# The first two weight units and x arrive in parts from two issuing queues and are rounded block by block; two more units are split before x's squares and the Silu table

## The chip, the cores and the metric

One core of one Trainium2 chip runs the whole program. The metric is the device time of one execution in microseconds (us); the kernel before takes 1129.0 us, the median of three runs.

## The reference, cut to what matters

Two transformer blocks in float32 on 256 rows of 1024 features. The change touches only the very first operation, a SwiGLU feed-forward layer behind an RMS norm:

```python
def rmsnorm(x, g):
    xf = x.astype(jnp.float32)
    y = xf * lax.rsqrt(jnp.mean(xf * xf, axis=-1, keepdims=True) + EPS)
    return y.astype(x.dtype) * g

def swiglu(x, w_gate, w_up, w_down):
    return (jax.nn.silu(x @ w_gate) * (x @ w_up)) @ w_down

h = h + 0.5 * rmsnorm(swiglu(rmsnorm(h, ffn1_pre_g[l]), ffn1_w_gate[l], ffn1_w_up[l], ffn1_w_down[l]),
                      ffn1_post_g[l])
```

with `w_gate` and `w_up` of 1024 x 2816 and `w_down` of 2816 x 1024. Behind it stand a state-space and an attention branch, a second feed-forward layer, and a second block with two attentions and a third such layer. The change leaves all of that as it is.

## The kernel before

**Split products.** Every float32 operand of a large product is held as two float32r parts, high (a rounded copy, made by ScalarE, ACT below) and low (the rest, made by VectorE, DVE below). A product is then three matmuls: high by high, high by low, low by high. The weights come in 180 *units* of 128 x 2048 values (1 MB each), which stand in a ring of five slots. For each unit SyncE (SP) issues the load into RAW (`load`, L363), ACT writes the high part WH (`split_hi`, L454, 461) and DVE the low part WL (`split_lo`, L1007, 1014); WL lies over RAW. A slot is loaded again once TensorE (PE) has counted the unit in `w_used`. Each engine runs its own instructions strictly in order, so their order in the text decides what waits for what.

**The first layer.** Unit 0 holds rows 0 to 511 of the first 256 columns of `w_gate` and `w_up` (two loads of 512 KB), as four row blocks k of 128 x 512; unit 1 holds rows 512 to 1023 of the same columns. Units 2 and 3 are the next 256 columns of gate and of up, unit 4 is the first 256 rows of `w_down`; then gate, up and down follow in turn.

**The start.** x lies in H as two row tiles t of 128 rows. For each tile and each half q of its features PE transposes four blocks (`turn_normed`, L1610, 1621); ACT multiplies them by the norm's gain into the high part XTH (`x_hi`, L612, 617) and DVE makes the low part XTL (`x_lo`, L1188, 1194). Both signal only after the last of the four. Four such quarters, (t, q) = (0, 0), (0, 1), (1, 0) and (1, 1), fill XT. PE's `first_norm` (L1867) multiplies: unit 0 by tile 0, block by block (12 matmuls, with tile 1's two transposes between), unit 0 by tile 1 (12), unit 1 by tile 0 (12), unit 1 by tile 1 (12). ACT's order is table load, x quarters (0, 0) and (0, 1), unit 0, squares of tile 0, x quarter (1, 0), unit 1, x quarter (1, 1), squares of tile 1, the Silu table, unit 2. The squares (`h_rstd`, L474, 483 to 485) give each row's norm factor, which is applied behind the products (L523 on ACT, L1063 on DVE); the result, the first 256 hidden columns, is transposed on PE in `turn_hidden` (L1757, 1762; L1767 turns the row factors).

**The loop.** For each later step j of `ffn` (L1736) PE multiplies the gate unit by all rows, as two blocks of 16 matmuls (`block`, L1740: L1753 with 512 columns, L1755 with 256), then the up unit likewise, then the down unit of the step before (24 matmuls, L1695 to 1697). In step 1 `turn_hidden` stands between the two blocks of unit 2. ACT splits units 3 and 4 around the copy of the turned hidden values (L527), and unit 5 behind them.

## Time and profile before

| | |
|---|---|
| runs | 1129.0, 1130.46 and 1128.63 us, median 1129.0 |
| the profiled execution | 1128.79 us, span 1127.0 us |
| PE busy | 1110.2 us (99% of the span) |
| DVE busy | 772.7 us (69%) |
| ACT busy | 618.7 us (55%) |
| DMA | 202.28 MB, 179 GB/s over the span |

A row of the timeline gives the start, the duration, the engine, the line and operation, what it writes and reads, how many were merged (x8), and in brackets the idle time of the engine before it and what ended that. Names ending in q are an engine's queue of DMA issues. Operations of an engine overlap a little: the next starts before the duration of the last is over, so that the pace is read from starts. The times of the table are the device's; those of the rows count from the span's first instruction.

### The profile page before, as it was taken

What the parts mean: (1) busy time and instruction counts of PE and PEld (TensorE: products, weight loads), DVE (VectorE), ACT (ScalarE), POOL (GpSimd) and SP (SyncE); (2) the same over time, 40 slices, a digit from 0 to 9 for tenths busy, and PEclk for the clock granted to TensorE, in tenths of its full rate; (3) what the DMA queues carried; (4) which work ended last, traced back from release to release, by engine and by line L of the source; (5) the groups of instructions that cost most, each with busy time, mean ns of one, the idle gap of its engine ahead of it and who ended that gap; (6) DMA issues with size and microseconds to landing.
All of it is one profiled execution on the core that took longest, in us unless ns stands there. A gap on an engine that the chain in (4) does not pass through costs nothing.

```text
span 1127.0 us, 14916 instructions
## 1 busy us (share of the span) xinstructions
PE 1110.2 (99%) x6114; PEld 949.8 (84%) x6114; DVE 772.7 (69%) x904; ACT 618.7 (55%) x877; POOL 20.9 (2%) x34
## 2 busy tenths in 40 slices
PE   6999999999999999999999999999999999999997
PEld 5888888999999987788888888888878888888886
DVE  4766667676767777868768666675775667766664
ACT  6644445554567766655456444456766546444443
POOL 0000000000001100000000000000000000000000
PEclk9999999999999999999999999999999999999999
DMA  8765564755566545345565655545633445555550
GB/s 280 249 191 189 187 191 136 229 187 179 178 205 192 167 166 205 118 157 192 177 218 182 193 187 189 193 147 154 221 124 119 168 151 187 186 187 188 186 187 38
DMA packets 131395, 202.28 MB, mean 179 GB/s; under 512 B 4944, under 2 KB 98000, under 8 KB 131072
## 3 DMA queue, kind: packets, MB, share of 16 engines
q1 hardware_dynamic: 128656, 190.68, 52.1%
q0 software_dynamic: 2672, 10.65, 2.8%
q8 instruction: 49, 0.80, 0.3%
q14 instruction: 18, 0.15, 0.0%
HBM read 200.24 MB, written 1.08 MB: 179 GB/s over the span
## 4 chain that ended last, share of the span: by engine, by line
PE 93%; DVE 4%; ACT 2%; issue 1%; DMA 0%; SPq 0%; DVEq 0%; ACTq 0%
PE TOP L1753 20%; PE ACC L1695 14%; PE ACC L1697 13%; PE ACC L1696 13%; PE TOP L1755 10%; PE TOP L1695 5%; PE TOP L1697 4%; PE TOP L1696 4%; DVE WL L1014 1%; ACT WH L461 1%; PE ACC L1973 1%; PE TOP L1621 1%; PE TOP L2131 1%; PE TOP L1818 1%; PE TOP L2139 0%
## 5 line engine op out<-in xcount | busy, mean ns | idle before, releaser
L1014 DVE TENSOR_TENSOR WL<-RAW,WH 128x2048 fp32r<-128x2048 f32 (+2 forms) x180 | 406.5, 2263 | 108.6 <-ACT WH L461 108.1
L461 ACT ACTIVATE WH<-RAW 128x2048 fp32r<-128x2048 f32 (+2 forms) x180 | 339.1, 1890 | 73.2 <-DMA RAW<-in_ffn_w_gate 30.7
L1753 PE MATMUL TOP<-XT,WH 128*128 128x512 f32 x960 | 340.4, 399 | 0.0
L1755 PE MATMUL TOP<-XT,WL 128*128 128x256 f32 x960 | 269.5, 281 | 0.0
L1753 PEld LDWEIGHTS TOP<-XT,WH 128*128 128x128 f32 x960 | 180.4, 188 | 44.9 <-DVE WL L1014 0.5
L1755 PEld LDWEIGHTS TOP<-XT,WL 128*128 128x128 f32 x960 | 181.3, 189 | 1.0
L1695 PE MATMUL ACC<-WH,KTH 128*128 128x512 f32 (+1 forms) x452 | 179.3, 397 | 0.0
L1697 PE MATMUL ACC<-WH,KTL 128*128 128x512 f32 (+1 forms) x452 | 176.0, 389 | 0.0
L1696 PE MATMUL ACC<-WL,KTH 128*128 128x512 f32 (+1 forms) x452 | 175.5, 388 | 0.0
L506 ACT ACTIVATE SCR<-TOP 128x512 f32<-128x512 f32 x60 | 35.8, 596 | 165.7 <-PE TOP L1755 165.7
L1697 PEld LDWEIGHTS ACC<-WH,KTL 128*128 128x128 f32 x452 | 84.8, 188 | 18.5
L1695 PEld LDWEIGHTS ACC<-WH,KTH 128*128 128x128 f32 x452 | 84.9, 188 | 18.2 <-DVE KTL L1169 0.7
L1696 PEld LDWEIGHTS ACC<-WL,KTH 128*128 128x128 f32 x452 | 85.0, 188 | 15.6
L1047 DVE TENSOR_TENSOR SCR<-TOP,SCR 128x512 f32<-128x512 f32 x60 | 41.4, 691 | 79.6 <-ACT SCR L506 79.6
L1695 PE MATMUL TOP<-WH,XT 128*128 128x512 f32 (+1 forms) x200 | 80.2, 401 | 4.5 <-DVE WL L1204 3.3
L1697 PE MATMUL TOP<-WH,XT 128*128 128x512 f32 (+1 forms) x200 | 78.0, 390 | 0.0
L1696 PE MATMUL TOP<-WL,XT 128*128 128x512 f32 (+1 forms) x200 | 77.8, 389 | 0.0
L1695 PE MATMUL ACC<-XT,WH 128*128 128x256 f32 x208 | 60.0, 289 | 0.0
L1696 PE MATMUL ACC<-XT,WH 128*128 128x256 f32 x208 | 59.6, 286 | 0.0
L1697 PE MATMUL ACC<-XT,WL 128*128 128x256 f32 x208 | 59.5, 286 | 0.0
L1695 PE MATMUL ACC<-WH,XT 128*128 128x512 f32 (+1 forms) x144 | 56.3, 391 | 0.7 <-DVE WL L1014 0.6
L1697 PE MATMUL ACC<-WH,XT 128*128 128x512 f32 (+1 forms) x144 | 54.2, 377 | 0.0
(304 smaller groups left out, 1449.9 us busy)
## 6 DMA issues: line engine op xcount, KB each, us to landing
RAW<-in_w_in SPq DMA_DIRECT2D x50, 1024.0 KB, 5.2
RAW<-in_ffn_w_down SPq DMA_DIRECT2D x22, 1024.0 KB, 4.9
RAW<-in_ffn_w_gate SPq DMA_DIRECT2D x20, 1024.0 KB, 5.4
RAW<-in_ffn_w_up SPq DMA_DIRECT2D x20, 1024.0 KB, 5.4
RAW<-in_w_down SPq DMA_DIRECT2D x11, 1024.0 KB, 4.9
RAW<-in_w_gate SPq DMA_DIRECT2D x10, 1024.0 KB, 5.4
RAW<-in_w_up SPq DMA_DIRECT2D x10, 1024.0 KB, 5.3
RAW<-in_ssd_w_branch SPq DMA_DIRECT2D x8, 1024.0 KB, 4.8
```

The lines of the kernel that those rows point to most:

```text
L461: nc.scalar.activation(WH[:, s, 0:n], RAW[:, s, 0:n], ACT.Copy).then_inc(w_hi, 1)
L506: nc.scalar.activation(LOW[n], TOP[:, bank:bank + 2, TOK:2 * TOK], ACT.Copy).then_inc(low_kept, 1)
L1014: tt(WL[:, s, 0:n], RAW[:, s, 0:n], WH[:, s, 0:n].bitcast(F32), ALU.subtract).then_inc(w_lo, 1)
L1047: tt(by_block(dst), TOP[:, bank:bank + 2, 0:TOK], LOW[n], ALU.add).then_inc((gate_sum, up_sum)[n], 1)
L1621: ins = nc.tensor.transpose(PS[6 + q][:, k * P:(k + 1) * P], src[:, t, j * P:(j + 1) * P], IDENT)
L1695: mm(ps, stat_hi, mov_hi, start=first, stop=False)
L1696: mm(ps, stat_hi, mov_lo, start=False, stop=False)
L1697: return mm(ps, stat_lo, mov_hi, start=False, stop=last)
L1753: mm(PS[bank], WH[:, slot(c), ws], XT[:, k, :, :].rearrange("p u t -> p (u t)"), start=k == 0, stop=False)
L1755: ins = mm(PS[bank][:, TOK:2 * TOK], WL[:, slot(c), ws], XTH[:, k, :], start=False, stop=k == KD - 1)
L1818: ins = nc.tensor.transpose(PS[7][:, k * P:(k + 1) * P], src[:, t, (k0 + k) * P:(k0 + k + 1) * P], IDENT)
L1973: ins = mm(PS[3][:, e * SSD_P:(e + 1) * SSD_P], DECAY[n % 2][:, e, :], XDT[:, e * SSD_P:(e + 1) * SSD_P], start=True, stop=True)
```

## The change

- **Loads.** x's tile 0 comes as two halves of its features, unit 0 as four row blocks (gate and up part of each), unit 1 as two halves. SP issues the first half of x, the four gate blocks, x's tile 1 and unit 1. ACT, which issued no DMA before, issues the identity matrix, the gains, the four up blocks and the second half of x ahead of its table load. The bytes are the same.
- **Rounding in turn.** ACT and DVE treat block k of x's quarter (0, 0) and block k of unit 0 one after the other, each with its own signal; the four turned blocks lie in four PSUM banks. PE starts on a block when both parts of it are there.
- **Transposes.** Each quarter has a place of its own in PSUM (`x_turned_at`). Quarter (0, 1) is turned behind block 1, quarter (1, 0) behind block 3, and quarter (1, 1) behind the first half of unit 1's product with tile 0.
- **Order.** ACT's squares of both tiles, which stood before and behind x's quarters, come behind unit 2's split, and unit 3's split comes before the Silu table. In the first layer `turn_hidden` stands behind both blocks of unit 2.

```diff
+LOADS[0] = LOADS[1] = 0
...
-        x_loaded = [sem(f"x_loaded{t}") for t in range(NT)]
+        x_loaded = [[sem("x_loaded0_first"), sem("x_loaded0_second")], [sem("x_loaded1")]]
+        first_loaded = [sem(f"first_unit_loaded{k}") for k in range(4)]
+        second_loaded = [sem(f"second_unit_loaded{h}") for h in range(2)]
+        second_hi, second_lo, x_first = sem("second_unit_hi"), sem("second_unit_lo"), sem("first_rows_hi")
+        x_first_lo = sem("first_rows_lo")
         loaded, tab_loaded, stored = sem("loaded"), sem("tables_loaded"), sem("stored")
...
+        def x_turned_at(t, k):
+            if t == 0 and k < 4:
+                return PS[(6, 7, 2, 3)[k]][:, 0:P]
+            return PS[{(0, 1): 0, (1, 0): 1, (1, 1): 6}[t, k // 4]][:, k % 4 * P:(k % 4 + 1) * P]
...
-            sp.dma_start(H[:, 0, :], x_in[:, 0, :]).then_inc(x_loaded[0], 16)
-            sp.dma_start(IDENT, w["tables"][:, 0:P]).then_inc(ident_loaded, 16)
-            sp.dma_start(COLS[:, 0:KD], w["cols"][:, 0:KD]).then_inc(ident_loaded, 16)
+            sp.dma_start(H[:, 0, 0:512], x_in[:, 0, 0:512]).then_inc(x_loaded[0][0], 16)
+            for k in range(4):
+                sp.dma_start(RAW[:, 0, k * 512:k * 512 + 256],
+                             w["ffn1_w_gate"][k * P:(k + 1) * P, 0:256]).then_inc(first_loaded[k], 16)
+            sp.dma_start(H[:, 1, :], x_in[:, 1, :]).then_inc(x_loaded[1][0], 16)
+            for h in range(2):
+                part = RAW[:, 1, h * 1024:(h + 1) * 1024].rearrange("p (k c) -> p k c", c=512)
+                for n, src in enumerate((w["ffn1_w_gate"], w["ffn1_w_up"])):
+                    sp.dma_start(part[:, :, n * 256:(n + 1) * 256],
+                                 src[512 + 256 * h:768 + 256 * h, 0:256].rearrange("(k p) c -> p k c", p=P)
+                                 ).then_inc(second_loaded[h], 16)
...
                 nc.scalar.activation(KTH[:, half_of(0)], PS[3], ACT.Copy).then_inc(hT_hi, 1)
-                split_hi()
+                if f:
+                    split_hi()
...
-            def first_unit_hi():
-                act.wait_ge(raw[0], 16 * LANDED[next(splits)])
+            def first_hi_parts():
+                next(splits)
+                act.wait_ge(ident_loaded, 32)
+                act.wait_ge(xn_turned, 1)
                 for k in range(4):
+                    ins = nc.scalar.activation(XTH[:, k, 0:P], x_turned_at(0, k), ACT.Copy, scale=COLS[:, k:k + 1])
+                    ins.then_inc(x_first, 1) if k < 3 else ins.then_inc(xt_hi, 1)
+                    act.wait_ge(first_loaded[k], 32)
                     a = slice(k * 512, (k + 1) * 512)
                     ins = nc.scalar.activation(WH[:, 0, a], RAW[:, 0, a], ACT.Copy)
                     ins.then_inc(first_hi, 1) if k < 3 else ins.then_inc(w_hi, 1)
+            def second_unit_hi():
+                next(splits)
+                for h in range(2):
+                    act.wait_ge(second_loaded[h], 32)
+                    a = slice(h * 1024, (h + 1) * 1024)
+                    nc.scalar.activation(WH[:, 1, a], RAW[:, 1, a], ACT.Copy).then_inc(w_hi if h else second_hi, 1)
+            act.dma_start(IDENT, w["tables"][:, 0:P]).then_inc(ident_loaded, 16)
+            act.dma_start(COLS[:, 0:KD], w["cols"][:, 0:KD]).then_inc(ident_loaded, 16)
+            for k in range(4):
+                act.dma_start(RAW[:, 0, k * 512 + 256:(k + 1) * 512],
+                              w["ffn1_w_up"][k * P:(k + 1) * P, 0:256]).then_inc(first_loaded[k], 16)
+            act.dma_start(H[:, 0, 512:1024],
+                          w["x"].rearrange("o (t p) d -> p (o t) d", p=P)[:, 0, 512:1024]).then_inc(x_loaded[0][1], 16)
             ln_exp()
-            x_hi(0, 0)
+            first_hi_parts()
             x_hi(0, 1)
-            first_unit_hi()
+            x_hi(1, 0)
+            second_unit_hi()
+            x_hi(1, 1)
+            split_hi()
             h_rstd(0, 0)
-            x_hi(1, 0)
+            h_rstd(0, 1)
             split_hi()
-            x_hi(1, 1)
-            h_rstd(0, 1)
             nc.scalar.preload_act_table(ACT.Silu)
-            split_hi()
             ffn(0, U_FFN1)
...
-            def first_unit_lo():
+            def first_lo_parts():
                 next(splits)
+                dve.wait_ge(ident_loaded, 32)
                 for k in range(4):
+                    dve.wait_ge(x_first, k + 1) if k < 3 else dve.wait_ge(xt_hi, 1)
+                    ins = stt(XTL[:, k, 0:P], x_turned_at(0, k), COLS[:, k:k + 1], XTH[:, k, 0:P].bitcast(F32),
+                              ALU.mult, ALU.subtract)
+                    ins.then_inc(x_first_lo, 1) if k < 3 else ins.then_inc(xt_lo, 1)
                     a = slice(k * 512, (k + 1) * 512)
                     dve.wait_ge(first_hi, k + 1) if k < 3 else dve.wait_ge(w_hi, 1)
                     ins = tt(WL[:, 0, a], RAW[:, 0, a], WH[:, 0, a].bitcast(F32), ALU.subtract)
                     ins.then_inc(first_lo, 1) if k < 3 else ins.then_inc(w_lo, 1)
-            x_lo(0, 0)
+            def second_unit_lo():
+                next(splits)
+                for h in range(2):
+                    dve.wait_ge(w_hi, 2) if h else dve.wait_ge(second_hi, 1)
+                    a = slice(h * 1024, (h + 1) * 1024)
+                    tt(WL[:, 1, a], RAW[:, 1, a], WH[:, 1, a].bitcast(F32), ALU.subtract).then_inc(w_lo if h else second_lo, 1)
+            first_lo_parts()
             x_lo(0, 1)
-            first_unit_lo()
             x_lo(1, 0)
+            second_unit_lo()
+            x_lo(1, 1)
             split_lo()
-            x_lo(1, 1)
             split_lo()
             ffn(0, U_FFN1)
...
+            def turn_input(t, q):
+                pe.wait_ge(x_loaded[t][-1 if t else q], 16)
+                if t and q:
+                    pe.wait_ge(xt_lo, 1)
+                for k in range(4 * q, 4 * q + 4):
+                    ins = nc.tensor.transpose(x_turned_at(t, k), H[:, t, k * P:(k + 1) * P], IDENT)
                 ins.then_inc(xn_turned, 1)
...
                     block(c, 0, 6)
-                    if j == 1:
+                    if j == 1 and f:
                         turn_hidden()
                     block(c, 1, 7).then_inc(w_used, 1)
+                    if j == 1 and not f:
+                        turn_hidden()
...
             def first_norm(c):
                 for k in range(4):
-                    pe.wait_ge(first_lo, k + 1) if k < 3 else pe.wait_ge(w_lo, c + 1)
-                    pe.wait_ge(xt_lo, 1)
+                    if k < 3:
+                        pe.wait_ge(first_lo, k + 1)
+                        pe.wait_ge(x_first_lo, k + 1)
+                    else:
+                        pe.wait_ge(w_lo, c + 1)
+                        pe.wait_ge(xt_lo, 1)
                     half(c, 0, 0, 4, (k,))
-                    if k % 2:
-                        turn_normed(0, 1, k // 2)
+                    if k == 1:
+                        turn_input(0, 1)
+                turn_input(1, 0)
                 pe.wait_ge(xt_lo, 3)
                 half(c, 0, 1, 5).then_inc(w_used, 1)
+                pe.wait_ge(second_lo, 1)
+                pe.wait_ge(xt_lo, 2)
+                half(c + 1, 1, 0, 4, (0, 1))
+                turn_input(1, 1)
                 pe.wait_ge(w_lo, c + 2)
-                half(c + 1, 1, 0, 4).then_inc(chunk_half, 1)
+                half(c + 1, 1, 0, 4, (2, 3)).then_inc(chunk_half, 1)
                 pe.wait_ge(xt_lo, 4)
                 half(c + 1, 1, 1, 5).then_inc(w_used, 1)
             pe.wait_ge(ident_loaded, 32)
-            first_tile(0)
+            turn_input(0, 0)
```

**ACT, from the program's start to the splits behind x's quarters, before** (XT is x's high part, WH the weights', SS the sums of squares):

```order
L472 ACT_TABLE_LOAD
L617 ACTIVATE XT<-TOP,COLS 128x128 x8
L626 ACTIVATE WH<-RAW 128x512 x4
L483 ACTIVATE SCR,SS<-H 128x1024
...
L617 ACTIVATE XT<-TOP,COLS 128x128 x4
L461 ACTIVATE WH<-RAW 128x2048
L617 ACTIVATE XT<-TOP,COLS 128x128 x4
...
L638 ACT_TABLE_LOAD
L461 ACTIVATE WH<-RAW 128x2048
L523 ACTIVATE SCR<-TOP,RS 128x256 x2
```

**The same stretch of ACT now** (between the first pair of block and unit block and the last stand two more such pairs):

```order
L666 DMA RAW<-in_ffn_w_up 128x256 x4
L668 DMA H<-in_x 128x512
L492 ACT_TABLE_LOAD
L648 ACTIVATE XT<-TOP,COLS 128x128
L652 ACTIVATE WH<-RAW 128x512
...
L638 ACTIVATE XT<-ACC,COLS 128x128 x8
L661 ACTIVATE WH<-RAW 128x1024 x2
L638 ACTIVATE XT<-TOP,COLS 128x128 x4
L481 ACTIVATE WH<-RAW 128x2048
...
L481 ACTIVATE WH<-RAW 128x2048
L680 ACT_TABLE_LOAD
L544 ACTIVATE SCR<-TOP,RS 128x256 x2
```

Seven DMA issues (two of them are those of the identity and the gains) stand ahead of the table load. The last quarter of x (the row L638 with x4) stands ahead of unit 2's split (the first L481); the squares stand between the two L481, and the second L481 is unit 3.

**PE, around the second product of unit 0, before** (WH and WL with XT are products, TAB with H are transposes):

```order
L1697 MATMUL TOP<-WH,XT 128x512
L1621 MATMUL TOP<-TAB,H 128x128 [waits xt_lo,x_loaded1]
L1621 MATMUL TOP<-TAB,H 128x128 x3
L1695 MATMUL TOP<-WH,XT 128x512 [waits xt_lo,first_unit_lo]
...
L1695 MATMUL TOP<-WH,XT 128x512 [waits xt_lo,weights_lo]
L1696 MATMUL TOP<-WL,XT 128x512
L1697 MATMUL TOP<-WH,XT 128x512
L1621 MATMUL TOP<-TAB,H 128x128 [waits xt_lo,x_loaded1]
L1621 MATMUL TOP<-TAB,H 128x128 x3
L1695 MATMUL TOP<-WH,XT 128x512 [waits xt_lo]
```

**PE, the same place and unit 1's first product now:**

```order
L1754 MATMUL TOP<-WH,XT 128x512 [waits xt_lo,weights_lo]
L1755 MATMUL TOP<-WL,XT 128x512
L1756 MATMUL TOP<-WH,XT 128x512
L1680 MATMUL ACC<-TAB,H 128x128 [waits x_loaded1]
L1680 MATMUL ACC<-TAB,H 128x128 x3
L1754 MATMUL TOP<-WH,XT 128x512 [waits xt_lo]
...
L1754 MATMUL TOP<-WH,XT 128x512 [waits xt_lo,second_unit_lo]
...
L1680 MATMUL TOP<-TAB,H 128x128 [waits xt_lo,x_loaded1]
L1680 MATMUL TOP<-TAB,H 128x128 x3
L1754 MATMUL TOP<-WH,XT 128x512 [waits weights_lo]
```

Before, the transposes of quarter (1, 0) had six products and another four transposes between them and the product that waits for that quarter (`xt_lo`). Now they stand directly ahead of it. The transposes of quarter (1, 1) have moved behind six products of unit 1.

## Rows read from the trace of the kernel before

**Rows 1.** The page's busy times, and PE's longest wait past 20 us.

```profile
PE 1110.2 (99%) x6114; PEld 949.8 (84%) x6114; DVE 772.7 (69%) x904; ACT 618.7 (55%) x877; POOL 20.9 (2%) x34
PE ACC L1695 <- DVE WL L1014: 0.6, 1, 0.6
```

**Rows 2.** The timeline of PE, 0 to 32 us.

```profile
4.83 1.97 PE L1621 MATMUL TOP<-TAB,H 128*128 128x128 f32 x8 [4.83 <-DMA COLS<-in_cols]
10.12 0.80 PE L1695 MATMUL TOP<-WH,XT 128*128 128x512 f32 x1 [3.31 <-DVE WL L1204]
...
15.14 0.60 PE L1621 MATMUL TOP<-TAB,H 128*128 128x128 f32 x4
16.42 0.50 PE L1695 MATMUL TOP<-WH,XT 128*128 128x512 f32 x1 [0.68 <-DVE XT L1194]
19.32 0.50 PE L1695 MATMUL TOP<-WH,XT 128*128 128x512 f32 x1
...
25.09 0.50 PE L1753 MATMUL TOP<-XT,WH 128*128 128x512 f32 x1
27.97 0.60 PE L1762 MATMUL ACC<-TAB,SCR 128*128 128x128 f32 x4
28.54 0.48 PE L1753 MATMUL TOP<-XT,WH 128*128 128x512 f32 x1
31.44 0.40 PE L1753 MATMUL TOP<-XT,WH 128*128 128x512 f32 x1
```

**Rows 3.** The chain of waits from 0 to 32 us: start, duration, what.

```profile
4.83 1.13 PE TOP L1621 x4
6.05 1.15 ACT XT L617 x4
9.46 0.61 DVE WL L1204
12.62 0.43 PE TOP L1697
14.00 1.15 ACT XT L617 x4
16.92 0.23 PE TOP L1696
```

**Rows 4.** The timeline of ACT.

```profile
8.47 2.19 ACT L626 ACTIVATE WH<-RAW 128x512 fp32r<-128x512 f32 x4 [0.24 <-DMA RAW<-in_ffn_w_up]
17.82 1.11 ACT L483 ACTIVATE SCR<-H 128x1024 f32<-128x1024 f32 x1
19.50 1.28 ACT L638 ACT_TABLE_LOAD   x1
20.79 1.92 ACT L461 ACTIVATE WH<-RAW 128x2048 fp32r<-128x2048 f32 x1
```

**Rows 5.** The timeline of DVE.

```profile
22.74 2.29 DVE L1014 TENSOR_TENSOR WL<-RAW,WH 128x2048 fp32r<-128x2048 f32 x1 [2.44 <-ACT WH L461]
49.13 0.69 DVE L1047 TENSOR_TENSOR SCR<-TOP,SCR 128x512 f32<-128x512 f32 x1 [2.13 <-ACT SCR L506]
```

**Rows 6.** The timeline of SP's queue, seventh to ninth issue.

```profile
3.69 0.43 SPq L370 DMA_DIRECT2D RAW<-in_ffn_w_gate  x1
4.17 0.78 SPq L370 DMA_DIRECT2D RAW<-in_ffn_w_up  x1
4.99 0.97 SPq L370 DMA_DIRECT2D RAW<-in_ffn_w_gate  x1
```

**Rows 7.** DMA issues by line: count, KB each, us from issue to landing.

```profile
H<-in_x SPq DMA_DIRECT2D x1, 512.0 KB, 3.6
RAW<-in_ffn_w_up SPq DMA_DIRECT2D x1, 512.0 KB, 5.9
H<-in_x SPq DMA_DIRECT2D x1, 512.0 KB, 6.6
COLS<-in_cols SPq DMA_DIRECT2D x1, 4.0 KB, 3.1
```

More of the change, by code:

```diff
@@ L384, in ffn_loads @@
                 for n, (kind, j) in enumerate(FF):
-                    if kind == "d":
+                    if u0 == U_FFN1 and n < 2:
+                        pass
+                    elif kind == "d":
                         load(u0 + n, down[j * 256:(j + 1) * 256, :], D)
@@ L390, in ffn_loads @@
                         gate_up(u0 + n, "ab".index(kind), j, gate, up)
-                    if u0 == U_FFN1 and n == 0:
-                        sp.dma_start(H[:, 1, :], x_in[:, 1, :]).then_inc(x_loaded[1], 16)
                     if u0 == U_FFN1 and n == 6:
@@ L478, in h_rstd @@
                 else:
-                    act.wait_ge(x_loaded[t], 16)
+                    for part in x_loaded[t]:
+                        act.wait_ge(part, 16)
                 own.wait() if own.n else None
@@ L612, in x_hi @@
             def x_hi(t, q):
-                act.wait_ge(ident_loaded, 32)
                 act.wait_ge(xn_turned, 2 * t + q + 1)
                 for k in range(4 * q, 4 * q + 4):
-                    ins = nc.scalar.activation(XTH[:, k, t * P:(t + 1) * P], PS[6 + q][:, k % 4 * P:(k % 4 + 1) * P],
-                                               ACT.Copy, scale=COLS[:, k:k + 1])
+                    ins = nc.scalar.activation(XTH[:, k, t * P:(t + 1) * P], x_turned_at(t, k), ACT.Copy,
+                                               scale=COLS[:, k:k + 1])
                 ins.then_inc(xt_hi, 1)
-            def first_unit_hi():
-                act.wait_ge(raw[0], 16 * LANDED[next(splits)])
+            def first_hi_parts():
+                next(splits)
+                act.wait_ge(ident_loaded, 32)
+                act.wait_ge(xn_turned, 1)
                 for k in range(4):
+                    ins = nc.scalar.activation(XTH[:, k, 0:P], x_turned_at(0, k), ACT.Copy, scale=COLS[:, k:k + 1])
+                    ins.then_inc(x_first, 1) if k < 3 else ins.then_inc(xt_hi, 1)
+                    act.wait_ge(first_loaded[k], 32)
                     a = slice(k * 512, (k + 1) * 512)
@@ L1069, in ffn @@
                 nc.vector.tensor_copy(RSB, PS[2][:, 0:TOK]).then_inc(rsb_ok, 1)
-                split_lo()
+                if f:
+                    split_lo()
                 dve.wait_ge(rsb_ok, f + 1)
@@ L1610, in turn_normed @@
             def turn_normed(n, t, q):
[L1612 to L1615 removed]
+                pe.wait_ge(xn_ok, 4 * (n - 1) + 2 * t + q + 1)
                 if t:
                     pe.wait_ge(xt_lo, 4 * n + q + 1)
[L1618 removed]
                 for k in range(4):
                     j = 4 * q + k
[L1621 removed]
+                    ins = nc.tensor.transpose(PS[6 + q][:, k * P:(k + 1) * P], XN[:, t, j * P:(j + 1) * P], IDENT)
+                ins.then_inc(xn_turned, 1)
+            def turn_input(t, q):
[4 more added lines that the diff above has]
+                    ins = nc.tensor.transpose(x_turned_at(t, k), H[:, t, k * P:(k + 1) * P], IDENT)
                 ins.then_inc(xn_turned, 1)
```

11 lines of the change are left out of this document (2 added, 9 removed).

## The prediction

> **What bounds the kernel now.** I read the page's busy times first: PE works 1110.2 of 1127.0 us [rows 1]. So nearly any time comes from what PE waits for, and the list of PE's waits says where that is: its longest wait past the first 20 us is 0.6 us [rows 1]; the rest is at the start. There the timeline of PE shows three gaps [rows 2]: 4.83 us until the gains (COLS) have landed, 3.31 us between the transposes and the first product at 10.12 us, and 0.68 us at 16.42, before unit 0's second product. At 25.09 the loop's first block starts, and unit 3 at 31.44. The chain of waits then says what fills the second gap [rows 3]: ACT's quarter of x (1.15 us), DVE's quarters, and the low part of one unit block (0.61 us). From 31.44 on nothing is changed but PE's start and how far ACT and DVE are behind it. So the question is one number: when does PE start unit 3?
>
> **To the first product.** The gains are now ACT's second DMA. SP's eighth issue starts at 4.17 [rows 6], the first at 0.74, which is 0.49 us each; so the gains are issued at about 1.2 and land 3.1 us later [rows 7], at 4.3. The first half of x is half of a transfer that landed after 3.6 us [rows 7], and is there too. PE starts at 4.3 instead of 4.83. ACT must first issue seven DMAs, until 0.74 + 7 x 0.49 = 4.17, and load its table, 1.28 us [rows 4]: ready at 5.45. The four transposes take 1.22 us (4.83 to 6.05 in the chain [rows 3]): 5.52. The two meet almost exactly, and ACT starts on x at 5.5, against 6.05.
>
> Then one block of x (a quarter of 1.15 us), one block of unit 0 (2.19 us for four [rows 4], so 0.55), its low part and the hand-over (9.46 to 10.12 [rows 2, 3], 0.66), and about 0.1 us for the wait between: PE's first product starts at 5.5 + 0.29 + 0.55 + 0.1 + 0.66 = 7.1. That is 3.0 us earlier. The next blocks follow every 0.87 us on DVE (0.27 for x, 0.6 for the unit), while PE needs 1.28 us for the three matmuls of a block at 0.43 each [rows 3], so PE is not held again here.
>
> Have the data landed by then? The loads share one stream of bytes, so I go by bytes: x's tile 0 (512 KB) landed at 0.74 + 3.6 = 4.34; with the identity and both parts of unit 0, 1.6 MB had landed at 2.59 + 5.9 = 8.5 [rows 7]. On the line between these two, block 0 (complete with 580 KB) lands at 4.6 and block 3 (1.35 MB) at 7.5; if parts lag behind their bytes, up to 1 us later. ACT wants them at 5.8 and 8.2. Close, but within the line. x's second half is wanted at 9.8 and comes by about 9; x's tile 1, issued by SP at about 3.1 as before, lands 6.6 us later [rows 7] and is wanted at 12.1.
>
> **To unit 0's second product.** PE does the same twelve matmuls and four transposes as before, and those of the next quarter: 10.12 to 15.14 [rows 2] is 5.02 us, with PE's clock at its lower level for the first part: steps of 0.43 us for 512 columns are 1.2 GHz, and the later ones of 0.23 are 2.4 GHz [rows 3]. The clock rose about 3.4 us after 10.12. I take the same course from the new start. Quarter (1, 0) is then turned from 7.1 + 5.0 = 12.1 to 12.7 (0.60 us [rows 2]). Here is the price of the new order. Before, that quarter's way over ACT and DVE (14.00 to 16.42 [rows 2, 3], 2.42 us) ran beside six products and four transposes, and PE stood 0.68 us. Now nothing stands between: ACT starts at 12.8, and PE resumes at 15.2. PE idles 2.5 us. Of the 3.0 us won, 1.2 are left.
>
> **To unit 2.** Twelve matmuls take 2.8 us (24 from 19.32 to 24.9 [rows 2], 0.23 each): 18.0. Unit 1's two halves are split well before (ACT 13.9 to 15.9). Six matmuls of unit 1: 19.4. Only now quarter (1, 1) is turned, and ACT, in order, has waited for it since 15.9. ACT gets it at 20.0, is through at 21.15, and only then starts unit 2: 1.92 us [rows 4] and DVE's 2.29 us [rows 5] end at 25.4 to 25.5. Before, ACT started unit 2 at 20.79 [rows 4]. PE for its part finishes six matmuls at 21.3, waits for the quarter until 20.0 + 2.42 = 22.4, and ends at 25.3. It starts unit 2 at 25.5, where it started at 25.09. **The lead is gone, and 0.4 us with it**: a whole quarter and a whole unit's split now hang in series behind a late transpose.
>
> **To unit 3.** Behind unit 2's split ACT has two rounds of squares of 1.7 us (17.82 to 19.50 with the two small steps [rows 4]), unit 3 (1.82), and the table (1.28): 23.1 + 3.4 + 1.8 + 1.3 = 29.6. Two scaled copies and DVE's two products bring the hidden values to 31.4. PE has both blocks of unit 2 behind it at 25.5 + 2.88 + 2.8 = 31.2 [rows 2] and waits 0.2 us. The transposes take 0.57 us (27.97 to 28.54) as before: unit 3 starts at 32.0 instead of 31.44. Had the transposes stayed between the blocks, PE would have stood 3 us; the move of them is worth that, and is counted. The split of unit 3 before the table costs nothing on PE: its low part is ready at 30.5.
>
> **Behind it.** DVE comes out of the squares' delay late: unit 4's low part ends at 34.4, the turned hidden values and row factors at 35.4. PE wants them at 32.0 + 5.65 = 37.6. So 2 us of cover are left, and DVE, which waited 2.13 us before the next sum [rows 5], catches up. I cost this at nothing; if it failed, what it costs is the overrun alone.
>
> **The sum.** +0.6 us at unit 3, and nothing later. The profiled execution took 1128.79 us (its span and 1.8 us around it), 0.2 below the median of 1129.0. So 1128.79 + 0.6 = **1129.4 us**. A measurement of this kernel can tell about 0.2%, 2.3 us, from no change: within that the change is none.
>
> A rule that speaks against this change in itself: the Trainium skill, page "DMA: Bandwidth & Descriptors", section "Issuing engines are not separate DMA queues", says that DMAs of several issuing engines run on the same 16 engines and that a second issuer saves only the sequencer's time. By that rule the second queue is worth at most the issues that it takes off SP; the trace of before has one issuer and can't show it.
>
> **The rivals.**
> - *ACT's issues are slow* (the other side, slower). SP's eighth and ninth issue took 0.78 and 0.97 us [rows 6]. Above 0.50 us each, the table load ends behind the transposes, and each further 0.1 us costs 0.7 us, undiminished, since the whole chain to unit 2 hangs on it. At 0.80 us each: table ready at 7.6, +2.1 us, 1131.5 us. Against it: SP's first seven kept to 0.49 with fewer bytes in flight. 10%.
> - *The parts land late.* Even 4 KB took 3.1 us [rows 7], so small transfers save little, and two queues share the engines. Blocks 0.3 to 1 us later give 1129.7 to 1130.4. 15%. The same page's section "Bandwidth" says that small transfers run at a fraction of the rate of one of 1 MB, which points this way.
> - *The clock rises sooner.* PE now stands 1.6 us between transposes and products instead of 3.3. If it multiplies at 2.4 GHz from the start, six matmuls save 0.2 us each, the transposes 0.35 and the fill 0.2, together 1.7 us. They go through to unit 2: 1127.7 us. 12%.
> - *The clock stays or falls low in the new gap* of 2.5 us. Eighteen matmuls at 0.43 instead of 0.23 are +3.6 us, half of that if it recovers midway: 1131.2 to 1133. Against it: the gap of 0.68 us left the clock up; none of this length stands behind a rise in the trace. 8%.
> - *The lead survives.* If the late quarter didn't hold unit 2 (its hand-over shorter than the 2.42 us of before), unit 2 could start at PE's own end without gaps, 1.2 to 2 us earlier: 1127.5 us. 7%.
>
> **How the numbers follow.** My forecast has 48%, with 1128.8 to 1130.2 as its own range (starts spread by the clock's rise). From 1127.5 (the two faster cases) to 1131.2 (late parts, and the lower part of the slow cases) about 17% is left out. Faster by over 0.2% (below 1126.8) needs two of the gains at once: 6%. Slower by over 0.2% (above 1131.2): half of the slow issues and most of the low clock, 12%. Within: 82%.
>
> **What would show it.** In the profile after, in this order: the first transpose at 4.3; ACT's table load ending by 5.5; the first product near 7.1; a gap of PE of about 2.5 us before unit 0's second product, released by DVE's low part of x; ACT idle some 4 us until about 20 for the last quarter; a gap of 1.1 us on PE before unit 1's second product; unit 2 at 25.5, a short gap before `turn_hidden`, and unit 3 at 32.0. A table load that ends after 6, steps of 0.43 us behind the gap, or unit 3 before 31 would prove me wrong.

## The result and the profile after

The changed kernel takes **1131.82 us** (median of 16 executions, 1128.48 to 1136.77); the kernel before, timed beside it, 1128.91 us (16 executions). The ratio is 1.0023, with a 95% interval of 1.0015 to 1.0031: slower by some 2.9 us, where 0.6 was forecast. The range ended at 1131.2.

The profiled execution took 1131.33 us (span 1129.7). The page's busy times and the list of PE's waits, after:

```profile
PE 1111.9 (98%) x6114; PEld 950.7 (84%) x6114; DVE 773.0 (68%) x905; ACT 619.0 (55%) x878; POOL 20.9 (2%) x34
PE TOP L1680 <- DMA COLS<-in_cols: 4.4, 1, 4.4
PE TOP L1754 <- DVE XT L1235: 3.4, 2, 2.4
PE TOP L1754 <- DVE WL L1250: 2.0, 1, 2.0
```

Before, the start cost PE 4.8, 3.3 and 0.7 us of waiting, 8.8 together [rows 2]. Now it costs 4.4, 2.0 and 3.4, which is 9.8: all that the early product won is waited for again behind it, and 1 us more. Besides, PE is busy for 1.7 us longer than before [rows 1], with the same 6114 matmuls. Two causes, then: waiting, and a lower clock. The timeline of PE after, for [rows 2]:

```profile
4.38 0.69 PE L1680 MATMUL TOP<-TAB,H 128*128 128x128 f32 x2 [4.38 <-DMA COLS<-in_cols]
...
7.48 0.79 PE L1754 MATMUL TOP<-WH,XT 128*128 128x512 f32 x1 [1.98 <-DVE WL L1250]
...
10.50 1.12 PE L1680 MATMUL ACC<-TAB,H 128*128 128x128 f32 x4
...
12.96 0.60 PE L1680 MATMUL ACC<-TAB,H 128*128 128x128 f32 x4
...
15.95 0.50 PE L1754 MATMUL TOP<-WH,XT 128*128 128x512 f32 x1 [2.39 <-DVE XT L1235]
...
20.19 0.60 PE L1680 MATMUL TOP<-TAB,H 128*128 128x128 f32 x4
...
23.18 0.50 PE L1754 MATMUL TOP<-WH,XT 128*128 128x512 f32 x1 [0.99 <-DVE XT L1235]
...
26.14 0.50 PE L1812 MATMUL TOP<-XT,WH 128*128 128x512 f32 x1
...
31.90 0.60 PE L1821 MATMUL ACC<-TAB,SCR 128*128 128x128 f32 x4
...
32.48 0.48 PE L1812 MATMUL TOP<-XT,WH 128*128 128x512 f32 x1
```

PE multiplies 2.64 us earlier (7.48 against 10.12), has 0.47 us left at unit 0's second product (15.95 against 16.42), is 1.05 us late at unit 2 (26.14 against 25.09) and 1.04 us late at unit 3 (32.48 against 31.44). The timeline of ACT after, for [rows 4], shows how the late transposes hold unit 2:

```profile
4.08 1.28 ACT L492 ACT_TABLE_LOAD   x1 [4.08 <-issue]
...
9.41 0.63 ACT L652 ACTIVATE WH<-RAW 128x512 fp32r<-128x512 f32 x1 [0.60 <-DMA RAW<-in_ffn_w_up]
11.66 1.14 ACT L638 ACTIVATE XT<-ACC,COLS 128x128 fp32r<-128x128 f32 x4 [1.62 <-PE ACC L1680]
...
20.83 1.14 ACT L638 ACTIVATE XT<-TOP,COLS 128x128 fp32r<-128x128 f32 x4 [4.20 <-PE TOP L1680]
21.84 1.93 ACT L481 ACTIVATE WH<-RAW 128x2048 fp32r<-128x2048 f32 x1
```

ACT stands idle 4.20 us for the quarter that PE turns at 20.19, and unit 2, for which it needs nothing from PE, waits behind it: 21.84, where it began at 20.79 before [rows 4].

The other 1.7 us lie far behind the change. Stretches of 10 us before (first two rows) and after (last two): the number ahead of the DMA share (0.93, 0.90) is the granted clock of PE as a share of 2.4 GHz. (Ahead of the clock's first rise this column shows 1.00, although the steps of 0.43 us for 512 columns are those of 1.2 GHz. The mean clocks of the executions agree with this column, so they don't count that time either; there the clock is read from the steps.)

```profile
210.00:220.00 10.00, 10.00 (x63) 9.18 (x62) 7.03 (x9) 6.25 (x8) 0.00 (x0) 0.93 0.68 225
220.00:230.00 10.00, 10.00 (x78) 10.00 (x78) 9.22 (x25) 5.66 (x7) 0.00 (x0) 0.90 0.61 197
```

```profile
210.00:220.00 10.00, 10.00 (x53) 8.73 (x53) 5.25 (x4) 4.21 (x4) 0.00 (x0) 0.84 0.44 140
220.00:230.00 10.00, 10.00 (x73) 10.00 (x73) 8.46 (x27) 7.22 (x10) 0.00 (x0) 0.83 0.72 218
```

There, behind a unit whose products are only 32 columns wide, the clock went down from 2.4 to 1.2 GHz once before (0.07 x 10 + 0.10 x 10 = 1.7 us lost) and twice after (1.6 + 1.7 = 3.3 us). PE never idles in these stretches. 1.0 us from the start and 1.7 us from here make up the whole difference of the two spans, 2.7 us.

But this profile is one execution. Is the second low stretch the change's doing? The experiments speak against it: what the change does to the clock happens in the start, and this profile happens not to show it.

### The profile page after: what moved, and what is told of

Read it like the earlier page. It is cut to its first block, busy times and chain, and to the rows that moved or that the text cites. A ratio compares the mean times of both kernels' runs of the same rounds, so it can differ in the third digit from the quotient of the medians.

```text
span 1129.7 us, 14922 instructions
## 1 busy us (share of the span) xinstructions
PE 1111.9 (98%) x6114; PEld 950.7 (84%) x6114; DVE 773.0 (68%) x905; ACT 619.0 (55%) x878; POOL 20.9 (2%) x34
## 4 chain that ended last, share of the span: by engine, by line
PE 92%; DVE 3%; ACT 2%; issue 1%; DMA 1%; ACTq 0%; DVEq 0%
PE TOP L1812 20%; PE ACC L1754 14%; PE ACC L1756 13%; PE ACC L1755 13%; PE TOP L1814 10%; PE TOP L1754 5%; PE TOP L1755 4%; PE TOP L1756 4%; DVE WL L1055 1%; ACT WH L481 1%; PE ACC L2043 1%; PE TOP L2201 1%; DMA H<-in_x 1%; PE TOP L1671 1%; PE TOP L1879 1%
## 5 line engine op out<-in xcount | busy, mean ns | idle before, releaser
L481 ACT ACTIVATE WH<-RAW 128x2048 fp32r<-128x2048 f32 (+2 forms) x179 | 337.3, 1889 | 71.6 <-DMA RAW<-in_ffn_w_gate 29.7
```

The lines of the kernel that those rows point to most:

```text
L481: nc.scalar.activation(WH[:, s, 0:n], RAW[:, s, 0:n], ACT.Copy).then_inc(w_hi, 1)
```

## The experiments

The theory at first: the late transposes (PE order) hold unit 2, and the lower clock is what the new times of things do to the narrow products. Rivals: the second queue delivers its parts late; the new gap of 2.4 us lets the clock fall in the start. The table holds every run, with what its profile shows at three places: the start of unit 3 (in kernels that keep `turn_hidden` between unit 2's blocks it is left out), whether the granted clock fell in the first 40 us after its first rise, and how many low stretches there are between 210 and 230 us. Each ratio is to the kernel before, timed in the same set of runs (medians of 1128.5 to 1128.9 us). All ratios lie within 1% of 1; what is told apart here are tenths of a percent, and only where the intervals do it.

| run | median us (executions) | ratio, 95% interval | span | unit 3 | fell in the start | low at 210 to 230 |
|---|---|---|---|---|---|---|
| before | 1129.0 (3) | | 1127.0 | 31.44 | no | 1 |
| after | 1131.82 (16) | 1.0023, 1.0015 to 1.0031 | 1129.7 | 32.48 | no | 2 |
| a_again | 1132.85 (4) | 1.0038, 1.0025 to 1.0052 | 1131.2 | 36.54 | yes | 0 |
| a_third | 1132.94 (10) | 1.0035, 1.0022 to 1.0048 | 1134.7 | 37.41 | yes | 2 |
| b_mixed | 1129.62 (12) | 1.0009, 0.9996 to 1.0022 | 1128.1 | | no | 0 |
| a_mixed | 1133.71 (7) | 1.0029, 1.0015 to 1.0043 | 1132.4 | 36.18 | yes | 0 |
| b_late_gains | 1131.32 (11) | 1.0018, 1.0009 to 1.0026 | 1129.5 | | no | 1 |
| a_turn_early | 1130.52 (12) | 1.0001, 0.9989 to 1.0013 | 1126.0 | 30.36 | no | 1 |
| a_filled | 1133.51 (6) | 1.0032, 1.0020 to 1.0044 | 1132.7 | 35.55 | no | 1 |
| a_one_queue | 1131.22 (10) | 1.0012, 1.0002 to 1.0021 | 1126.6 | 32.20 | no | 0 |
| a_hold | 1131.55 (10) | 1.0018, 1.0009 to 1.0027 | 1129.8 | 33.79 | yes | 1 |
| a_swap | 1127.25 (11) | 0.9980, 0.9970 to 0.9989 | 1124.4 | 29.84 | no | 0 |
| a_swap_again | 1125.60 (11) | 0.9977, 0.9965 to 0.9988 | 1123.9 | 29.26 | no | 0 |
| a_swap_one_queue | 1129.08 (11) | 0.9998, 0.9989 to 1.0007 | 1127.9 | 32.27 | no | 1 |
| a_swap_x_on_act | 1128.26 (12) | 1.0000, 0.9991 to 1.0009 | 1127.1 | 30.91 | no | 1 |
| b_late_turn | 1136.45 (4) | 1.0072, 1.0054 to 1.0090 | 1134.8 | | yes | 2 |
| a_hidden_between | 1136.91 (4) | 1.0065, 1.0049 to 1.0082 | 1134.8 | | twice | 1 |

The columns add up: 1127.0 + (unit 3 - 31.44) + 1.7 x (low stretches - 1) gives the span of ten of the eleven rows with a start of unit 3 (a_mixed, whose later products differ, left aside) within 0.8 us, and that of a_filled within 1.6. So between unit 3 and the end the number of low stretches is the only large difference; the up to 0.8 us that is left (1.6 in a_filled) stays open.

**The narrow products, taken out.** In both kernels the narrow matmuls (`beside`) were put between wide ones, in small groups:

```diff
-                    half(c + 1, 1, 0, 4).then_inc(chunk_half, 1)
-                    pe.wait_ge(w_lo, c + 3)
-                    beside(0)
...
+                        pe.wait_ge(w_lo, c + 3)
+                        for k in range(4):
+                            ins = half(c + 1, 1, 0, 4, (k,))
+                            if k == 3:
+                                ins.then_inc(chunk_half, 1)
+                            beside(0, (2 * k, 2 * k + 1))
```

> The kernel before, with the 48 narrow products (32 columns) of the dt unit mixed among the wide ones of unit 1 of the mixer instead of standing in two blocks of 24. If the low clock near 220 us comes from those two blocks (theory 1), its profile shows no low stretch there and its runs gather near 1127 us, 1.7 us below the kernel before. If the low stretch is chance or belongs to another place (theory 2), time and clock stay as before, 1128.9 us, 0.998.

> The changed kernel with the same mixing. Theory 1: the clock stays high, the runs lose their spread, and what is left against the kernel before with the same mixing is the start alone, +0.8 to +1.0 us: about 1128 us. Theory 2 (the 2.7 us all come from the start or from the queues): it stays near 1131.8 us.

Neither profile has a low stretch at 210 to 230 us. One profile each doesn't show that the mixing did it, since four profiles without it (a_again, a_one_queue, a_swap, a_swap_again) have none there either. The mean clocks say more: 8 of b_mixed's 12 executions have 0.999 or 1.000, against 5 of 30 of the kernel before in the same set. But two of the twelve have 0.993 and are 6 us longer (1135.4 and 1135.8 us); where the clock fell in them no profile shows. The kernel before stays level instead of the 1.7 us faster that were expected: the narrow products had covered the split of the next unit, and the list of PE's waits of b_mixed has a new one, whose longest part stands directly ahead of them:

```profile
PE TOP L1713 <- DVE WL L1014: 1.7, 2, 1.5
205.28 0.47 PE L1713 MATMUL TOP<-WH,XT 128*128 128x512 f32 x1 [1.54 <-DVE WL L1014]
```

The changed kernel doesn't come closer: 4.1 us above b_mixed (1133.71 against 1129.62). So the second low stretch of the profile after was not the cause. Of a_mixed's seven executions two have a span of 1128.4 and 1128.5 us at a mean clock of 0.999, five have 1131.1 to 1133.0 at 0.998. The profiled one (1132.4) is of the five, and its clock fell in the start, behind the gap. A fall costs 1.7 us, so it can explain less than half of the 4 us between the two groups. The rest is lost in another way, and the next two profiles show how that can be.

**The changed kernel once more**, unchanged, in two other sets of runs:

> The changed kernel once more, for a second profile and more runs on the chip of this call. Theory 1: another trace may show a low stretch within the first 25 us; unit 2 starts between 25.9 and 28. Theory 2: none does, and the clock differs from run to run only by the stretches near 210 and 220 us.

> The changed kernel a third time, for one more profile of its start. From the profiles so far: the up blocks land 4.9 or 6.5 us after their issue, and the clock falls back in the gap in about two executions of three; unit 2 then starts at 26, 27 or 30 us.

Both profiles show what the first did not. PE's timeline of a_third, two stretches of 2 us in it, and two rows of a_again:

```profile
10.14 0.80 PE L1754 MATMUL TOP<-WH,XT 128*128 128x512 f32 x1 [1.12 <-DVE WL L1250]
...
12.37 1.12 PE L1680 MATMUL ACC<-TAB,H 128*128 128x128 f32 x4 [0.57 <-DMA H<-in_x]
...
15.84 1.05 PE L1680 MATMUL ACC<-TAB,H 128*128 128x128 f32 x4
19.29 0.50 PE L1754 MATMUL TOP<-WH,XT 128*128 128x512 f32 x1 [2.39 <-DVE XT L1235]
...
28.12 0.50 PE L1754 MATMUL TOP<-WH,XT 128*128 128x512 f32 x1 [1.01 <-DVE XT L1235]
...
37.27 0.38 PE L1826 MATMUL ACC<-TAB,RS 128*128 128x128 f32 x2
```

```profile
20.00:22.00 2.00, 2.00 (x7) 1.57 (x6) 1.50 (x2) 0.00 (x0) 0.00 (x0) 0.55 0.16 64
22.00:24.00 2.00, 2.00 (x7) 1.51 (x7) 0.00 (x0) 0.00 (x0) 0.00 (x0) 0.60 0.02 6
```

```profile
14.91 0.63 PE L1756 MATMUL TOP<-WH,XT 128*128 128x512 f32 x1
15.34 0.68 PE L1680 MATMUL ACC<-TAB,H 128*128 128x128 f32 x4
```

First, block 1 and x's second half come late: quarter (0, 1) is turned at 12.37 (a_again: 11.87), at 10.50 in the first profile. Second, the clock's first rise comes late too. In the first profile the steps are at 0.23 us from 11.80 on, 4.3 us behind the first product. In a_again they stand at 0.43 up to the transposes at 15.34, 8.2 us behind it, and in a_third the same four transposes still take 1.05 us at 15.84. The six products and four transposes from quarter (0, 1) to quarter (1, 0) so take 3.5 us in both instead of 2.5 (12.96 - 10.50). What sets the rise wasn't tested. In both profiles PE had stood 0.6 to 1.1 us twice since its first product, but in a_swap_again (below), where it stood for nothing, the steps are also at 0.43 us up to 12.97, 5.7 us behind the first product. Third, the clock is at 1.2 GHz behind the gap of 2.39 us: 0.45 x 2 + 0.40 x 2 = 1.7 us. Together unit 3 starts 5 to 6 us later than before, 4.1 and 4.9 us later than in the first profile. Of these the fall is 1.6 to 1.7 us; most of the rest is the late parts and the late rise, which together cost more than the fall in these two profiles.

**A later start alone.** In the kernel before, identity and gains issued behind unit 0's loads:

```diff
                     if u0 == U_FFN1 and n == 0:
+                        sp.dma_start(IDENT, w["tables"][:, 0:P]).then_inc(ident_loaded, 16)
+                        sp.dma_start(COLS[:, 0:KD], w["cols"][:, 0:KD]).then_inc(ident_loaded, 16)
...
-            sp.dma_start(IDENT, w["tables"][:, 0:P]).then_inc(ident_loaded, 16)
-            sp.dma_start(COLS[:, 0:KD], w["cols"][:, 0:KD]).then_inc(ident_loaded, 16)
```

> The kernel before with the identity and the gains issued behind unit 0's loads, so that the whole program from the first transpose on starts about 0.9 us later, nothing else moved. If a later start alone brings the second low stretch near 210 us (the phase is tied to the start of the program), +2.6 us and clock 0.996. If the phase is free from run to run, +0.9 us and the same share of low stretches as before.

The shift came out larger than meant: the 4 KB of gains, issued behind 1 MB of weights, landed only at 7.9 us instead of 4.8. Everything moved by 3 us and the kernel lost 2.4, but the mean clock of its executions (0.9984) was no lower than that of before (0.9977). Here being late cost its own time, and the clock didn't fall more often.

**The order of the transposes.** Three kernels change it. a_turn_early turns quarter (1, 1) right behind (1, 0); a_swap also exchanges quarters (1, 0) and (0, 1) on PE, ACT and DVE, so that a whole product stands between the transposes and the product that waits for them (PE's part of the edit of a_swap; ACT and DVE take the two quarters in the same order):

```diff
                     if k == 1:
-                        turn_input(0, 1)
-                turn_input(1, 0)
-                pe.wait_ge(xt_lo, 3)
+                        turn_input(1, 0)
+                turn_input(0, 1)
+                turn_input(1, 1)
+                pe.wait_ge(xt_lo, 2)
                 half(c, 0, 1, 5).then_inc(w_used, 1)
...
-                turn_input(1, 1)
```

> The changed kernel with the last quarter of x turned directly behind quarter (1, 0), not behind six products of unit 1. If the late transpose holds unit 2 (my reading), ACT has no gap of 4.2 us, PE none before unit 1's second product, unit 2 starts at 24.4 instead of 26.2 and unit 3 at 30.7 instead of 32.5: 1.8 us less. If it doesn't hold it, less than 0.3 us.

> The changed kernel with quarters (1, 0) and (0, 1) of x exchanged on PE, ACT and DVE, and quarter (1, 1) turned right behind them, ahead of unit 0's second product. If order alone costs the lead: PE has no gap from the first product at 7.3 to unit 2, which starts at 22.0 to 22.5 instead of 26.2 (before 25.1); unit 3 at 28.4 instead of 32.5 (before 31.4): about 3 us faster than the kernel before, 1125.9 us. If something else takes the lead (late loads of units 2 and 3, the squares behind unit 2), the gain shrinks to 1 us or less.

> The kernel of a_swap once more, unchanged, in five rounds. It was the only one of the study that stood below the kernel before (ratio 0.9980, interval 0.9970 to 0.9989), and the kernel with the same order but the parts of x on ACT's queue stood level with it. If the order of the quarters is what counts (no idle TensorE of over 2 us between its first quarters, so no fall of the granted clock there, and unit 2 some 1.5 us earlier than in the kernel before), the ratio comes out at 0.997 to 0.999 again and the start of the profile shows a granted clock of 1.00 throughout. If the first result was a chance of where the low stretches near 210 to 225 us fell, it comes out at 0.9995 to 1.001.

a_turn_early took back 1.3 us of the median of after, enough to stand level with the kernel before. In its profile unit 3 starts at 30.36, 2.1 us before that of after: the late quarter did hold unit 2, and ACT no longer waits for it. Its gap is 1.96 us, and the clock did not fall:

```profile
15.85 0.50 PE L1754 MATMUL TOP<-WH,XT 128*128 128x512 f32 x1 [1.96 <-DVE XT L1235]
```

a_swap has no gap over 0.4 us behind its first product, and is **faster than both kernels**, in two sets of runs (both intervals end below 1). PE's timeline of a_swap_again:

```profile
9.98 1.05 PE L1680 MATMUL ACC<-TAB,H 128*128 128x128 f32 x4
...
13.34 0.60 PE L1680 MATMUL ACC<-TAB,H 128*128 128x128 f32 x4
13.78 0.60 PE L1680 MATMUL TOP<-TAB,H 128*128 128x128 f32 x4
...
17.47 0.50 PE L1754 MATMUL TOP<-WH,XT 128*128 128x512 f32 x1 [0.35 <-DVE WL L1259]
...
23.04 0.39 PE L1812 MATMUL TOP<-XT,WH 128*128 128x512 f32 x1
...
29.12 0.38 PE L1826 MATMUL ACC<-TAB,RS 128*128 128x128 f32 x2
```

Of the three gaps behind the first product 0.35 us is left; unit 2 starts at 23.04, 2.05 us before that of the old kernel, and unit 3 at 29.26, 2.2 us before. The ratio of 0.9977 is 2.6 us. The 3 us that were expected were not quite reached: unit 3 was to start at 28.4 and came at 29.84 and 29.26.

The reverse, in the kernel before: (1, 0) turned directly ahead of its product, (1, 1) behind it.

```diff
-                    if k % 2:
-                        turn_normed(0, 1, k // 2)
+                turn_normed(0, 1, 0)
...
                 half(c, 0, 1, 5).then_inc(w_used, 1)
+                turn_normed(0, 1, 1)
```

> The kernel before with one thing of the change alone: quarter (1, 0) is turned directly ahead of the product that waits for it (and quarter (1, 1) behind that product). Loads, rounding and queues as before. If the new gap is the order's doing, PE stands 2.4 us ahead of unit 0's second product instead of 0.7, and the later split of unit 2 puts unit 2 at 29.4 (+4.3 us). If such a gap makes the clock fall back in part of the executions, the profile or the runs' mean clock show one low stretch more than the kernel before (0.9978 falls by 0.001); if not, the clock stays.

It is the slowest but one of the study, 8 us above before. In its profile unit 2 starts 5.0 us later than before (0.8 of that lies ahead of the first product, which waits longer for its data); the rest is the clock, whose mean over its four executions is 0.995, against 0.998 of the kernel before in the same set. Its two rows:

```profile
18.23 0.50 PE L1695 MATMUL TOP<-WH,XT 128*128 128x512 f32 x1 [2.52 <-DVE XT L1194]
...
30.04 0.50 PE L1753 MATMUL TOP<-XT,WH 128*128 128x512 f32 x1 [2.80 <-DVE WL L1014]
```

The gap of 2.52 us left the clock up; the one of 2.80 us, in which PE waits for unit 2 itself, did not: the granted clock is 0.50 from 32 to 34 us. So the order alone, with the old loads and one queue, brings both the gap and a fall.

**Filling the gap.** Nine matmuls on data that is there, their result not used, in after's gap:

```diff
                 turn_input(1, 0)
+                for _ in range(9):
+                    mm(PS[7], XTH[:, 0, 0:P], WH[:, 0, 0:512], start=True, stop=True)
                 pe.wait_ge(xt_lo, 3)
```

> The changed kernel with nine extra matmuls (their result is read by nobody) put into PE's wait ahead of unit 0's second product; order and waits unchanged. Theory 1, the clock falls back in that gap of 2.4 us in some executions: unit 2 starts at 26.2 as in the changed kernel, but no low stretch follows the start, the mean clock of the runs rises from 0.9966 towards the 0.9977 of the kernel before, and the median falls by 0.8 to 1.7 us. Theory 2, all low stretches are those near 210 and 220 us: median and clock stay, 1131.8 us.

```profile
16.29 2.66 PE L1942 MATMUL TOP<-WH,XT 128*128 128x512 f32 x9
```

The profile shows no fall. By itself that says little, since two of the seven profiles with the open gap show none either. The mean clocks of all executions say more: 0.9975 over its six, near that of before in the same set (0.9978), where a_again had 0.9962 over four. The nine matmuls took 2.7 us (16.29 to 19.03) in place of the wait of 2.39, since the first of them ran at 1.2 GHz; x's parts were as late as in a_again (quarter (0, 1) at 12.11). So unit 3 came 1.0 us before a_again's, not 1.7, and the medians of the two (1133.51 and 1132.85) don't show even that. As a test of the clock it speaks for the theory, as a cure it is none.

**The queues.** a_one_queue issues everything on SP. a_hold keeps both, but lets SP wait until unit 0's parts and x's first tile have landed before it issues the rest.

```diff
+            for k in range(4):
+                sp.wait_ge(first_loaded[k], 32)
+            sp.wait_ge(x_loaded[0][1], 16)
             sp.dma_start(H[:, 1, :], x_in[:, 1, :]).then_inc(x_loaded[1][0], 16)
```

> The changed kernel with all loads issued by SP again, in the order first half of x, identity, gains, blocks (gate and up in turn), second half of x. If the second queue carries the early start, the last parts are issued 2.4 us later and the first product comes 0.5 us or more later than 7.3; the total rises by as much. If the bytes set the landing, the first product stays within 0.3 us, and x's second half (which landed at 10.5) comes no later.

> The changed kernel, but SP issues x's tile 1 and unit 1 only when unit 0's parts and x's second half have landed. If the parts on ACT's queue are late because SP's later loads share the engines with them, they now land 3 to 4 us after their issue instead of 5.1 to 6.8, x's second half lands by 8.5 instead of 10.5 to 11.9, and block 1 is not waited for; x's tile 1 then lands at 12 or later and may delay quarter (1, 0). If ACT's queue is slow by itself, the landings stay.

The DMA rows of after (issues, KB each, median us from issue to landing), for [rows 7]:

```profile
RAW<-in_ffn_w_gate SPq DMA_DIRECT2D x4, 128.0 KB, 4.2
RAW<-in_ffn_w_up ACTq DMA_DIRECT2D x4, 128.0 KB, 5.1
...
H<-in_x ACTq DMA_DIRECT2D x1, 256.0 KB, 6.9
...
COLS<-in_cols ACTq DMA_DIRECT2D x1, 4.0 KB, 3.2
```

and of a_one_queue:

```profile
RAW<-in_ffn_w_gate SPq DMA_DIRECT2D x4, 128.0 KB, 2.5
RAW<-in_ffn_w_up SPq DMA_DIRECT2D x4, 128.0 KB, 2.9
```

The same parts land in 2.5 and 2.9 us when one engine issues them in the order of their need, and in 4.2 and 5.1 us (a_again 6.5, a_third 7.0 for the up blocks) from two queues. The second queue does not bring the early start: with one the first product starts at 6.99, with two at 7.48 (7.19 to 7.64 in the other profiles of this order), though the last up block is issued only at 5.43. In a_hold they take 3.6 and 4.5 us, so a part of the delay comes from SP's later megabytes, which run beside ACT's small parts; PE waits for no block, but unit 1 is issued late and ACT waits for it. For the whole time neither kernel shows a gain: their intervals (1.0002 to 1.0021 and 1.0009 to 1.0027) overlap that of after. The Trainium skill, page "DMA: Bandwidth & Descriptors", section "Issuing engines are not separate DMA queues", has DMAs of all issuers interleave on the same engines and grants a second issuer the sequencer's time alone; these rows agree.

Both put together with a_swap's order:

> Both corrections together: x's quarters in the exchanged order and all loads from SP's queue. If the two losses are separate (order, 3 us; a second queue that delays the first parts, about 1 us), it is faster than the exchanged order alone: first product at 7.0, no wait for a late up block, unit 2 at 22.5 or before, about 1125.5 us. If they overlap, it equals the exchanged order, 1127 us.

> The exchanged order, with all of unit 0's parts on SP's queue and only the identity, the gains and x's later parts on ACT's. If parts on ACT's queue are late because they stand behind SP's traffic, the up blocks now land in 3 to 4 us, block 1 is not waited for, and x's tile 1, issued at 1.7 instead of 6.4, is there by 10: no wait at the transposes. Then 0.5 to 1 us faster than the exchanged order, 1126.5 us. If x on ACT's queue now takes the bandwidth of unit 0's parts, the first product moves to 8 or later and the gain is gone.

Neither helped; both are slower than a_swap, with intervals that at most touch (0.9989). With one queue x's tile 1 is issued only at 6.4 us (at 3.1 in after) and a_swap's order needs it early: PE stood 2.5 us for it at 12.57, while the clock was still low. With x's parts on ACT's queue and all weights on SP's, unit 3 started at 30.91, still 0.5 us ahead of before and 1.1 to 1.7 behind a_swap's two profiles, since block 1 came 0.87 us late and the steps stayed at 0.43 us up to 14.5. Its unit 0 parts took 4.4 and 5.1 us to land, although SP issued all of them: what delays them is what is under way beside them, whichever queue issued it. The order of the parts would have to be tuned for each order of the products; that was not followed up.

**The move of `turn_hidden`.** Put back between unit 2's blocks:

```diff
-                    if j == 1 and f:
+                    if j == 1:
                         turn_hidden()
                     block(c, 1, 7).then_inc(w_used, 1)
-                    if j == 1 and not f:
-                        turn_hidden()
```

> The changed kernel with the transposes of the hidden values back between the two blocks of unit 2. They need the squares, which now come later: PE stands about 2.7 us there, and the run takes 2.5 to 3 us more than the changed kernel, 1134.5 us. If something else covers the wait, less than 1 us.

PE stands 2.52 us there and the clock falls again right behind it. The row, and a stretch of 2 us:

```profile
34.16 1.11 PE L1821 MATMUL ACC<-TAB,SCR 128*128 128x128 f32 x4 [2.52 <-DVE SCR L1104]
...
34.00:36.00 2.00, 1.84 (x8) 1.75 (x9) 1.13 (x2) 1.64 (x3) 0.00 (x0) 0.50 0.77 282
```

The median is 4.0 to 5.1 us above those of the changed kernel, where 2.5 to 3 were expected; the wait and the fall together are 4.2. This part of the change is right, and with late squares it is needed.

## Why the prediction was wrong

Two steps failed: the clock's course from the new start, and the landing of the parts. The waits that the new order makes came within 0.2 us of the forecast, and they held unit 2 in the way that it gave.

- **The first product** was forecast at 7.1 and came at 7.48: ACT started on x 0.1 us late and on the first block of unit 0 another 0.2 (6.07), and the way from there to PE took 0.1 more. ACT's seven issues (table load at 4.08, forecast 4.17), the table (ready at 5.36, forecast 5.45) and ACT's start on x (5.60, forecast 5.5) stood. The rival of slow issues did not come true: they took 0.40 to 0.48 us each.
- **"Have the data landed by then?"** failed. x's second half was to come by 9; it landed at 10.46 in the first profile and at 11.8 and 12.3 us in the two others, and block 1 was 0.75 and 1.12 us late there. Interpolating by bytes took the two queues for one stream in order of need. That they share the engines with 1 MB and more of later loads was in the text, but only as a rival of 15%, for at most 1 us.
- **"PE idles 2.5 us"** was right to 0.1 (2.39), in every profile of this order. So was **"To unit 2"** in its mechanism: ACT idle 4.20 us for the last quarter, PE 0.99 us. What was passed on is the lateness of the start, 0.8 us at quarter (0, 1), of which the first product has 0.4 and PE's wait for x's second half 0.3. Unit 2 came at 26.14 instead of 25.5, unit 3 at 32.48 instead of 32.0. That was the forecast's +0.6 us, measured +1.04 in this profile.
- **"I take the same course from the new start"**, the clock's, is the step that failed by most. It took the rise from the trace of before and no fall behind it. Already the rise was another: the first step of 0.23 us comes 3.9 us behind the first product before, 4.3 in the first profile after, and the rise over 8 us behind it in a_again and a_third. In the new gap, or right behind it, the clock fell in five of seven profiles of kernels with this gap unfilled, at 1.7 us each. The rival had this mechanism and its size (up to 3.6 us, half if it recovers midway) but a chance of 8%: the trace of before had no gap over 0.68 us behind a rise, and I took the lack of a case for a reason against it.
- **The rest of the difference by the clock.** Over its 16 executions the changed kernel has a mean clock of 0.9966, the kernel before 0.9977 to 0.9983 in the sets of the study, about 0.998: 0.0014 x 1127 = 1.6 us. How much of it lies in the start is an estimate: five falls in seven profiles at 1.7 us make 1.2. The rest would be the low stretches at 210 to 230 us, which the prediction didn't speak of; a_turn_early, whose profile shows no fall in the start, also stands below the kernel before by mean clock (0.9972 against 0.9977, 0.6 us). Their number (0 to 2) goes up and down between profiles of kernels that are the same there; what sets it stays open. What is left of the 2.9 us is 1.3: the 0.6 of the forecast, and 0.7 for the late parts and the late rise.
- **"The move of them is worth that"**, some 3 us for `turn_hidden`: 2.5 us of waiting, confirmed. **"Behind it nothing"** held but for the low stretches: the sum of columns closes within 0.8 us (a_filled 1.6) with no further term. "So nearly any time comes from what PE waits for" is where the clock was lost from sight: the profile after has 1.7 us more of PE's busy time for the same 6114 matmuls.

## What to carry over

When a chain is made to start earlier, the transposes that feed a product must move up with it: place each producer one whole product ahead of its consumer on the in-order engine, or the gain is idled away and the clock may go with it. Where the trace has no gap of the length that a change will make, the fall of the clock behind it is an open price and belongs in the sum's range. Small urgent loads land late when large later ones are under way beside them. A second queue doesn't help against that; neither did a single queue win time in the end here, since the parts that it put off were needed too.

## What the chip showed that was not expected

- **Short gaps and the clock.** Of ten gaps of 2.39 to 2.80 us behind the clock's first rise in these profiles, seven were followed by a granted clock at half speed for 1.7 us of loss; the same gap of 2.39 us left it up in after and in a_one_queue. So did a gap of 2.52 us in b_late_turn. The nine profiles whose longest such gap was 0.3 to 2.0 us (before, b_mixed, b_late_gains, a_turn_early, a_filled and the four of the exchanged order) show no fall in the start. What decides between a fall and none at the same gap stays open.
- **A clock that falls with PE busy.** Behind the products of 32 columns it fell with PE 100% busy by the record, once before and twice after. With wide matmuls between them (b_mixed, a_mixed) the two profiles show no fall there, and most of b_mixed's executions a higher mean clock, but two of twelve a much lower one.
- **A small load behind large ones.** The gains (4 KB) took 3.1 us [rows 7] ahead of the weights; issued about 1 us later, behind 1 MB of weights, they landed 3.1 us later.
